# Seven tiles of the first LayerNorm: the normalised rows made by ACT instead of DVE, and the seats of the tile in front moved ahead of them

## The reference, cut to what matters

```python
def layer_norm(x, g, b):
    mu = jnp.mean(xf, axis=-1, keepdims=True)
    var = jnp.mean(jnp.square(xf - mu), axis=-1, keepdims=True)
    y = (xf - mu) * lax.rsqrt(var + LN_EPS) * g + b

h = layer_norm(ALPHA * h + jnp.einsum('bte,ed->btd', mix, w_out_l), ln1_g, ln1_b)   # "the first LayerNorm" of a layer
probs = softmax(h @ router_w)              # 16 experts in 4 groups; one group, then its top 2
# y += combine[:, e] * (silu(h @ w_gate[e]) * (h @ w_up[e])) @ w_down[e] for every e
h = layer_norm(ALPHA * h + y, ln2_g, ln2_b)
```

## Time and profile before

| what | value |
|---|---|
| median of 3 runs | 1070.32 us |
| the profiled execution's own time | 1070.91 us |
| its span, first to last instruction | 1069.1 us |
| PE busy | 952.4 us (89%) |
| DVE busy | 848.0 us (79%) |
| ACT busy | 658.9 us (62%) |
| POOL busy | 274.5 us (26%) |
| mean granted TensorE clock | 0.937 of full speed |

### The profile page before, as it was taken

One profiled execution on the slowest core, in us unless ns is written; L12 is line 12 of the kernel. 1 busy time (PEld: TensorE's weight loads), 2 busy tenths in 40 slices (PEclk: granted clock), 3 DMA queues, 4 the chain that ended last, 5 costly groups with the idle time before them and its releaser, 6 DMA issues. The chain is left out here.

```text
span 1069.1 us, 14977 instructions
## 1 busy us (share of the span) xinstructions
PE 952.4 (89%) x5010; PEld 786.0 (74%) x5010; DVE 848.0 (79%) x1198; ACT 658.9 (62%) x940; POOL 274.5 (26%) x323
## 2 busy tenths in 40 slices
PE   4999899989999999999249998989999999999940
PEld 4989677768888888887149996777788888888830
DVE  8867657879898989897595676486998989899936
ACT  5345431368888888887344454224888888888822
POOL 1223533344111111200171236231511121111005
PEclk9999889899999999999659998898999999999985
DMA  9423610789999999996550336138999999999514
GB/s 355 163 101 124 249 49 21 275 295 343 366 363 368 363 362 372 364 339 252 195 206 3 102 130 242 49 126 313 355 359 370 373 361 364 364 369 359 204 58 180
DMA packets 117116, 272.77 MB, mean 255 GB/s; under 512 B 8912, under 2 KB 11208, under 8 KB 117038
## 3 DMA queue, kind: packets, MB, share of 16 engines
q1 hardware_dynamic: 97408, 231.75, 59.9%
q10 hardware_dynamic: 9822, 24.48, 6.6%
q0 software_dynamic: 9824, 15.78, 4.0%
HBM read 266.51 MB, written 25.92 MB: 274 GB/s over the span
## 5 line engine op out<-in xcount | busy, mean ns | idle before, releaser
L1274 DVE TENSOR_TENSOR w_lo<-ring,w_hi 128x1024 fp32r<-128x1024 f32 x256 | 303.9, 1239 | 40.8 <-ACT w_hi L1670 38.2
L1670 ACT ACTIVATE w_hi<-ring 128x1024 fp32r<-128x1024 f32 x256 | 261.0, 1060 | 51.1 <-PE PS L944 27.0
L909 PE MATMUL PS<-w_hi,x_hi 128*128 128x512 f32 x512 | 164.5, 403 | 3.2 <-ACT w_hi L1670 3.0
L914 PE MATMUL PS<-w_lo,x_hi 128*128 128x512 f32 x512 | 163.4, 401 | 2.4 <-DVE w_lo L1274 2.4
L909 PE MATMUL PS<-w_hi,x_lo 128*128 128x512 f32 x512 | 161.7, 397 | 1.5 <-DVE x_lo L1264 1.5
L1281 DVE TENSOR_TENSOR w_lo<-ring,w_hi 128x1024 fp32r<-128x1024 f32 x128 | 155.7, 1223 | 8.9 <-ACT w_hi L1683 7.0
L1683 ACT ACTIVATE w_hi<-ring 128x1024 fp32r<-128x1024 f32 x128 | 134.8, 1059 | 28.6 <-PE PS L914 28.6
L1965 POOL DMA_INDIRECT M<-xs,idx x30 | 51.7, 1722 | 254.6 <-PE PS L890 228.6
L914 PEld LDWEIGHTS PS<-w_lo,x_hi 128*128 128x128 f32 x512 | 96.7, 190 | 27.0 <-DVE w_lo L1274 4.9
L909 PEld LDWEIGHTS PS<-w_hi,x_lo 128*128 128x128 f32 x512 | 97.3, 190 | 24.5 <-DVE x_lo L1264 1.9
L909 PEld LDWEIGHTS PS<-w_hi,x_hi 128*128 128x128 f32 x512 | 95.0, 191 | 24.5 <-issue 2.0
(11 more groups left out here) (219 smaller groups left out, 1647.4 us busy)
## 6 DMA issues: line engine op xcount, KB each, us to landing
ring<-in_w_gate SPq DMA_DIRECT2D x32, 2048.0 KB, 15.4
ring<-in_w_up SPq DMA_DIRECT2D x32, 2048.0 KB, 16.3
ring<-in_w_down SPq DMA_DIRECT2D x32, 2048.0 KB, 15.8
ring<-in_w_in SPq DMA_DIRECT2D x8, 2048.0 KB, 15.1
ring<-in_w_out SPq DMA_DIRECT2D x4, 2048.0 KB, 7.8
M<-in_cache_k ACTq DMA_DIRECT2D x8, 512.0 KB, 3.3
M<-in_cache_v ACTq DMA_DIRECT2D x8, 512.0 KB, 5.8
M<-ys ACTq DMA_DIRECT2D x4, 1024.0 KB, 6.0
```

The costliest lines, as they stand in the source:

```text
L909: pe.matmul(PS[:, n, :], x[:, c:c + P], w_hi[j][:, k * 512:(k + 1) * 512], start=(j == 0 and k == 0 and x is x_hi[par]), stop=False)
L914: mm = pe.matmul(PS[:, n, :], x_hi[par][:, c:c + P], lo[:, k * 512:(k + 1) * 512], start=False, stop=(j == 3 and k == 1))
L1274: dve.tensor_tensor(lo, w, w_hi[j][:, :].bitcast(F32), ALU.subtract).then_inc(up_lo, 1)
L1670: act.activation(w_hi[j][:, :], quarter(3 * par + n, j)[0], ACT.Copy).then_inc(up_hi, 1)
```

## The change

In the first LayerNorms z is no longer made by DVE. DVE writes minus the mean into column 0 of the tile's `stats`; POOL, after rstd, multiplies the two into column 1 and only then raises `ln_rstd`; ACT makes z = Identity(H * rstd + that bias) in one activation, in front of its own half of `turned_h`. On DVE the seats of the tile in front go where z was, then it waits for `z_done`, and `ln_h_gain` stands ahead of `turned_h` with every tile, the first too. The LayerNorm of the input and the second ones keep their z on DVE.

```diff
                 then(dve.bn_aggr(st[:, 12:14], st[:, 0:12]))
+                if q in LN1:
+                    dve.tensor_scalar(st[:, 0:1], st[:, 12:13], -1.0, None, ALU.mult)
                 dve.tensor_scalar(st[:, 14:15], st[:, 13:14], EPS, None, ALU.add).then_inc(ln_var, 1)
...
                     if n == 0 and l == 0:
                         o_scale(l, 12)
-                    ln_z(q, n)
-                    if n >= 1:
-                        ln_h_gain(q, n)
-                    turned_h(q, n)
-                    if n == 0:
-                        ln_h_gain(q, n)
-                    ln_h_shift(q, n)
                     if n >= 1:
                         seat(l, n - 1)
+                    dve.wait_ge(z_done, ln_count(q, n))
+                    ln_h_gain(q, n)
+                    turned_h(q, n)
+                    dve.wait_ge(ln_rstd, ln_count(q, n))
+                    ln_h_shift(q, n)
                     choose(l, n)
...
+            def ln_z(q, n):
+
+                j = order(q)[n]
+                rows = TN[j]
+                st = stats[0:rows, j, :]
+                act.wait_ge(ln_rstd, ln_count(q, n))
+                if 4 * q + n >= 2:
+                    act.wait_ge(hx_ps, 8 * q + 2 * n - 2)
+                act.activation(z_of(q)[n % 2][0:rows], H[0:rows, j, :], ACT.Identity, bias=st[:, 1:2],
+                               scale=st[:, 15:16]).then_inc(z_done, 1)
...
                     if n == last:
                         k_rows(l, (0, 1))
+                    ln_z(LN1[l], n)
                     turned_h(LN1[l], n)
...
-                pool.tensor_tensor(stats[p, j, 15:16], stats[p, j, 14:15], half[p, 0:1], ALU.pow
-                                   ).then_inc(ln_rstd, 1)
+                rstd = pool.tensor_tensor(stats[p, j, 15:16], stats[p, j, 14:15], half[p, 0:1], ALU.pow)
+                if q in LN1:
+                    then(rstd)
+                    rstd = pool.tensor_tensor(stats[p, j, 1:2], stats[p, j, 0:1], stats[p, j, 15:16], ALU.mult)
+                rstd.then_inc(ln_rstd, 1)
```

## The result

The changed kernel came to a median of 1075.14 us over 20 runs (1070.41 to 1082.0), the kernel before on the same chip to 1070.32: a ratio of 1.0047 with a 95% interval of 1.0028 to 1.0067. It is about 5 us slower, within the 1% that I called no change. The forecast was 1075.4 us. The number held, and the path of a middle tile is as forecast. But two of its terms came out smaller, and the rival with chance 0.10 (the clock falls) came true at another place and filled the gap, which was luck. The rest of this text is about that.

What follows compares the result with a forecast made beforehand. The path through z, transposes and logits, not the seats, was taken to bound the first-LayerNorm stages. Layer 0 +2.5 and layer 1 +2.6 sum to +5.1 us on the median 1070.32: 1075.4 us, range 1069.5 to 1080.

Steps and rivals of the forecast that it cites:

- the path of a middle tile: Middle tiles: statistics, power, z, transposes, logits, `choose`; +0.70 us each (0.09 mean, 0.27 product, 0.34 z on ACT).
- the clock falls: Layer 1's first tile: PE waits about 2 us for the turned half, clock falls; +4 us, 1079.4; chance 0.10.
- The seats worth nothing in a middle tile: Middle tiles: moving the seats on DVE gives 0 us, since they only fill time DVE had been waiting.
- The last tile of layer 0: z about 1.0 us later, also held by ACT's key copies; `first_x` no longer waits for seats; +0.38 us.
- The load in layer 1's first tile: Gain, now ahead of the turned half, waits for its load: +1.24 us, or -0.3 if the load is quick.
- The last tile of layer 1: Turned half comes 0.7 us later and the logits wait for it; `first_x` not held by seats; +0.66 us.
- the other tiles of layer 1: Layer 1 after its first tile: +0.70 us for the second tile, +0.66 us for the last.
- The rule on the shared ports: Skill's rule: 2-port DVE operations and GpSimd exclude each other; seats would hold POOL, 1077.9 us; forecast charged nothing.
- Rival 2: Seats on DVE hold POOL's power and product: 0.5 us in five tiles with seats, +2.5 us, 1077.9; chance 0.12.

Runs made afterwards that it cites:

- the filling alone: Kernel before, plus 6 and 24 unread transposes in PE's wait ahead of the last tile's `turn_z`, memset as before: median 1068.88 us, ratio 0.9983.
- filled, before: Kernel before with 6 and 24 unread transposes ahead of the last tile's `turn_z`, in two kernels: memset as before 1068.88 us, memset held until first z 1064.75 us.
- the filled change: Changed kernel plus 14 (layer 0) and 30 (layer 1) unread transposes in PE's wait ahead of the last tile's `turn_z`: median 1071.15 us, ratio 1.0016.

## Why the prediction was right, and where it was wrong

**The path of a tile: right.** +0.70 us forecast; R grew by 0.76, PE's round by 0.69. Its parts: 0.07 for minus the mean (0.09), 0.27 for the product (0.27, confirmed by leaving it out and doubling it), 0.43 for z (0.34; Identity with a bias per row took 0.09 more than the Copy of L1851, and no run separates the bias from the function). The seats worth nothing in a middle tile: shown by z on ACT in the old order.

**The last tile of layer 0: the path right, the clock behind it not counted.** `turn_z` came 3.2 us later relative to the first tile's residual (51.07 to 54.26; forecast 3.1), and `first_x` did not wait for seats, so that it was only 2.3 us late (forecast 2.5):

```profile
205.98 2.78 PE L843 MATMUL PS<-N,H 128*128 128x128 f32 x16
```

But x_hi was later by only 0.6 us: residual to x_hi was 64.13 us (64.21 in the second profile) against 63.55 (63.53 and 63.72). From `first_x` to x_hi it was 8.8, 8.8 and 9.0 us in the profiles of before and 7.1 and 7.2 in those of the change, because the clock was down for less of it (with the clock up all this way, in the kernel before with the filling alone, it was 7.3 us; in the kernel without the product, where it was down all this way, 11.0). Windows of PE in the second profile of before, whose `turn_z` starts at 201.34 us, and in the second of the change, at 204.61:

```profile
202.00:204.00 2.00, 2.00 (x25) 0.60 1.06 403
204.00:206.00 2.00, 1.08 (x9) 0.50 1.02 387
206.00:208.00 2.00, 2.00 (x11) 0.50 1.05 391
208.00:210.00 2.00, 2.00 (x15) 0.70 1.06 411
```
```profile
204.00:206.00 2.00, 1.39 (x14) 0.95 1.02 392
206.00:208.00 2.00, 1.80 (x23) 0.50 1.04 389
208.00:210.00 2.00, 2.00 (x14) 0.69 1.04 374
210.00:212.00 2.00, 1.95 (x23) 1.00 1.06 413
```

Yet PE's idle ahead of this `turn_z` had grown, from 0.99 to 1.95 us: here a longer idle did not bring a longer fall. With the same 1.95 us the kernel without the product has a fall of over 12 us, so at this place the idle does not settle it, and what does is not shown. Over all kernels this stretch from the first tile's residual to x_hi took 62.0 (filled, before) to 68.6 us (z on ACT in the old order): the clock moves it by more than the change does.

**The load in layer 1's first tile: wrong.** I took +1.24 us, "since the row is of this place". The row was one draw. With a gain that depends on the load, the wait ended 7.70 us after the residual in one profile of the change and 7.73 in the other, so the tile came out 0.3 us shorter, which was the other end of my bounds (residual to `choose`: 12.72 us before, 12.45 and 12.47 after). From issue to landing the load of the shift took 5.5 to 5.9 us in ten of the fourteen profiles and 7.0 to 7.1 in four, two of these the kernel before's first and third. Of the kernels in which the gain depends on it, the one with two products had it slow: its gain came 9.15 us behind the residual, and its tile took 13.88 us, 1.4 more than the change's, of which 0.3 belong to the second product. So the +1.24 us stood for the slow draw, and with the quick one the dependence still costs some 0.5 us against the order without it (11.98 in the kernel with z on ACT and the old order); z done without the memset beside it gives back more than that.

**The clock: the rival that came true, at another place.** I gave it 0.10, at the logits of the first tile, and argued from the row of 716 to 718 us that an idle PE keeps its clock. That row was one draw too: in the second profile of the same kernel the clock was down by the end of the same idle (0.60 as the mean of 714 to 716). The last tile of layer 1, where I had counted +0.66 us, has PE's longest idle in the two stages, and the +0.8 us that the change puts into it turned a short fall into one of 20 us and more. Its price, with T of 13.4 us as the mean of three profiles of before: 17.6 - 13.4 = 4.2 us. By the run times: the change lost 3.3 to 4.0 us when its idle was filled, and lengthening the idle alone cost 3.5 to 4.7.

**The sum.** By profiles, from the first tile's residual to x_hi in layer 1: 49.4 us before (three profiles: 48.36, 50.01, 49.96), 54.9 after (55.32, 54.47), +5.5, of which 1.3 are path and 4.2 clock; in layer 0 +0.6. Together that is 6.1 us, where the medians differ by 4.8. The forecast had 2.6 for layer 1 and 2.5 for layer 0. Term by term: 1.5 us too much for the load, 1.9 too much in layer 0, where the clock was down for less of the way than before, 0.2 too little for the other tiles of layer 1, and 4.2 us for the clock in layer 1 that the sum did not have at all. That these nearly cancel is luck; the number does not confirm the sum, only the parts that were tested singly. (One small slip in the sum: from the logits to `first_x` of layer 0 I added 0.66 us, where the row of the logits has 0.61; in the change it is 0.54.) The Trainium skill, TensorE: Matmul & The Clock Gate, "HAM oscillation — how this bites in real kernels", describes idle gaps of the engine that send its clock down and make what follows run cold. The traces of layer 1 agree with it in kind: behind 3.82 us of idle, with nothing else changed, T was 17.97 us instead of 12.31 to 13.96. I had looked at a falling clock as a risk for the stage's first tile and not asked which wait of PE was already the longest.

**The rule on the shared ports.** Rival 2 asked for 0.5 us in tiles with seats. In the tiles with seats the product took 0.18 to 0.19 us and the power 0.55 to 0.59, with the seats' instructions beside them: at most 0.04 us lost. What stretched a little was DVE's side: the last two instructions of the seats (L1225) took 0.50 to 0.57 us together in the four tiles of the change where the product stood beside them and 0.48 in the kernel without it, which is off the path. Where POOL's memset stood beside a DVE z of 128x1024 the exclusion was real, and holding the memset gave 1.45 us back.

**Open.** The kernel with z on DVE and seats first has a T of 18 us and R of 10.83 in its profiles, yet a median of 1069.4. Either most of its unprofiled runs don't have the long fall (3.40 us is the shortest idle with which it was seen; the mean granted clock of its nine unprofiled runs is 0.942, of its two profiled ones 0.927 and 0.936, of the change's twenty 0.933), or something later gives the time back. Only a profile shows the fall, and there are two of them. As long as this is open, the 4.2 us are shown for the profiles and only made likely for the medians.

## What to carry to other kernels

Ask of each engine's longest wait, and not only of the busiest engine, what the change adds to it: TensorE's wait of 2.98 us, made 0.8 longer, cost some five times that in the profiles, because the clock stayed down for the 20 us and more that followed. The wait ahead of layer 0's last `turn_z`, grown from 0.99 to 1.95 us, cost nothing of the kind in the two profiles of the change, so each wait has to be looked at by itself, in more than one profile. An operation moved to an idle engine is a gain only if the path doesn't go through it; here z went from a 0.81 us operation with one handoff to 1.24 us with a second operand to be made first, while the time freed on DVE had been a wait already. And a row that decides a term by the arrival of a transfer wants a second profile before it is taken at its value.

## What was not expected of the hardware

- On 128x1024, ACT's Identity with scale and bias per row takes 1.24 us, Copy with a scale per row 1.148 us (L1851), and a plain Copy that rounds 1.06 us (L1670).
- Granted clock at the last tile of layer 1: with the same work behind it, the fall at the end of 2.98 us of idle was over in some 3.4 us (two profiles), the one that goes with 3.40 to 4.07 us lasted 20 to 27 (eight profiles), though PE was busy for nearly all of it. It set in anywhere from 1.8 us before the idle's end to 1.2 us behind it. In the first profile of before a fall of 3.4 us came 5.2 us behind the start of `turn_z`; the filled change, with 0.48 us of idle, has one as well, 4.7 us behind it, so that this fall is not shown to come from the idle.
- Of the 77 runs of the kernel before, mean 1069.8 us, those with a mean clock lower by 0.01 were longer by 6.2 us (a straight line through them). At equal clock the change stands 2.5 us above that line, and 3.0 us of its mean difference of 5.5 go with its lower clock.
